# Down weights in whole 4 MB blocks, gate-up columns dealt to two column groups by eights

## The reference

```python
gu = jnp.dot(xb, w_gate_up[e]) + b_gate_up[e]          # 1024 -> 2048
glu = jnp.minimum(gu[:, ::2], SWIGLU_LIMIT)
lin = jnp.clip(gu[:, 1::2], -SWIGLU_LIMIT, SWIGLU_LIMIT)
act = glu * jax.nn.sigmoid(SWIGLU_ALPHA * glu) * (lin + 1.0)
y = jnp.dot(act, w_down[e]) + b_down[e]                 # 1024 -> 1024
```

## Time and profile before

| | |
|---|---|
| median of 3 runs | 1206.76 us (1205.69 to 1207.62) |
| the profiled execution | 1207.06 us, span 1205.3 us |
| mean granted clock of TensorE | 0.992 |
| TensorE busy / weight loads | 1148.6 us (95%) / 536.2 us |
| VectorE, ScalarE, GpSimd busy | 410.7, 208.5, 19.7 us |
| moved | 470.55 MB, mean 390 GB/s |
| chain that ended last | TensorE 68%, DMA 26%, VectorE 2% |

### The profile page before, as it was taken

One profiled execution on the slowest core, in us unless ns is written; L12 is line 12 of the kernel. 1 busy time (PEld: TensorE's weight loads), 2 busy tenths in 40 slices (PEclk: granted clock), 3 DMA queues, 4 the chain that ended last, 5 costly groups with the idle time before them and its releaser, 6 DMA issues.

```text
span 1205.3 us, 14952 instructions
## 1 busy us (share of the span) xinstructions
PE 1148.6 (95%) x6027; PEld 536.2 (44%) x6027; DVE 410.7 (34%) x798; ACT 208.5 (17%) x333; POOL 19.7 (2%) x40
## 2 busy tenths in 40 slices
PE   6999999999999999998989899999999999999997
PEld 4787889985333333332323233333333333333332
DVE  3547755673222232322222222222322323132222
ACT  3346644342010110101010101010101101010001
POOL 1000110000000000000000000000000000000000
PEclk9999999999999999999999999999999999999999
DMA  9997565699999999999999999999999999999994
GB/s 335 390 370 284 208 210 188 245 374 368 397 429 435 433 428 426 435 433 430 425 435 433 430 425 435 425 427 428 430 430 434 433 427 428 434 433 427 425 427 205
DMA packets 52546, 470.55 MB, mean 390 GB/s; under 512 B 4399, under 2 KB 9980, under 8 KB 31526
## 3 DMA queue, kind: packets, MB, share of 16 engines
q1 hardware_dynamic: 50308, 467.99, 93.5%
q10 hardware_dynamic: 2210, 2.16, 0.6%
HBM read 469.08 MB, written 1.06 MB: 390 GB/s over the span
## 4 chain that ended last, share of the span: by engine, by line
PE 68%; DMA 26%; DVE 2%; ACT 1%; issue 1%; SPq 1%; DVEq 0%; POOLq 0%; POOL 0%; ACTq 0%
PE ps L1059 22%; PE ps L828 15%; PE ps L1097 15%; DMA expert<-in_w_down 15%; DMA expert<-in_w_gate_up 11%; PE ps L1033 4%; PE ps L1004 2%; PE ps L772 2%; PE ps L703 1%; PE ps L985 1%; PE ps L1084 1%; ACT r_work L1299 1%; DMA ada_first<-in_w_ada 1%; DVE r_v L1740 1%; DVE r_v L1737 0%
## 5 line engine op out<-in xcount | busy, mean ns | idle before, releaser
L1059 PE MATMUL ps<-expert,r_work 128*64 128x512 f32 x2048 | 451.4, 595 | 7.4 <-DMA expert<-in_w_gate_up 6.6
L1059 PEld LDWEIGHTS ps<-expert,r_work 128*64 128x64 f32 x2048 | 147.1, 137 | 294.5 <-issue 281.4
L1097 PE MATMUL ps<-expert,r_work 128*64 128x512 f32 x1024 | 231.7, 603 | 23.4 <-DMA expert<-in_w_down 15.2
L1731 DVE TENSOR_SCALAR r_v<-ps 128x512 f32<-128x512 f32 x32 | 22.1, 692 | 366.4 <-PE ps L1059 366.4
L1097 PEld LDWEIGHTS ps<-expert,r_work 128*64 128x64 f32 x1024 | 72.7, 138 | 160.4 <-issue 135.8
L1295 ACT ACTIVATE r_v<-r_v 128x512 f32<-128x512 f32 x32 | 20.2, 630 | 706.5 <-DVE r_v L1731 706.5
L1408 DVE TENSOR_TENSOR w_lo<-stage,w_hi 128x2048 fp32r<-128x2048 f32 x36 | 82.8, 2306 | 55.3 <-ACT w_hi L1155 55.3
L1751 DVE TENSOR_TENSOR r_work<-ps,r_gb 64x512 f32<-64x512 f32 x64 | 44.1, 689 | 167.0 <-PE ps L1097 166.5
L828 PE MATMUL ps<-x_hi,w_hi 128*128 128x256 f32 x304 | 87.6, 288 | 0.0
L828 PE MATMUL ps<-x_lo,w_hi 128*128 128x256 f32 x304 | 86.0, 283 | 0.0
L828 PE MATMUL ps<-x_hi,w_lo 128*128 128x256 f32 x304 | 85.9, 283 | 0.0
(11 more groups left out here) (222 smaller groups left out, 866.5 us busy)
## 6 DMA issues: line engine op xcount, KB each, us to landing
expert<-in_w_gate_up SPq DMA_DIRECT2D x44, 4096.0 KB
expert<-in_w_down SPq DMA_DIRECT2D x64, 2048.0 KB, 18.4
expert<-in_w_gate_up SPq DMA_DIRECT2D x40, 2048.0 KB, 29.2
stage<-in_w_in SPq DMA_DIRECT2D x24, 1024.0 KB, 5.6
stage<-in_w_ada SPq DMA_DIRECT2D x16, 1024.0 KB, 7.1
ada_first<-in_w_ada SPq DMA_DIRECT2D x16, 256.0 KB, 6.4
ada_first<-in_w_ada SPq DMA_DIRECT2D x8, 512.0 KB, 11.9
stage<-in_w_o_attn SPq DMA_DIRECT2D x4, 1024.0 KB, 7.7
```

Source lines behind the costliest of these rows:

```text
L1059: mm = pe.matmul(ps[CAP * g:CAP * g + CAP, j, :], xg[:, 2 * (k % 4) + k // 4, :], buf[:, col:col + 512], start=False, stop=(k == KD - 1))
L1097: mm = pe.matmul(ps[CAP * half:CAP * half + CAP, 3, :], aT[:, ch, CAP * g:CAP * g + CAP], expert[n][:, col:col + 512], start=(q == 0), sto ...
```

## The change

The down weights of an expert are read with 32 KB runs in each partition: partition p now holds rows 8p to 8p + 7 of `w_down`, the first four in slot 4 and the last four in slot 5. In rounds 2 to 15 and 20 to 27 this is one load of 4 MB (`down_of_next`), issued when the whole down product of the round is done (`down_used` at 2i + 2); in the others two loads of 2 MB with runs of 16 KB stay, at their old moments. Both halves share one semaphore, and TensorE waits once, for all of the expert's down weights, before the first half of the product; the last expert alone keeps one semaphore for each half. In this row order group g must hold the features 8n + 4g + c, so the gate-up columns go to the groups by eights: the moving operand of a product is 64 runs of 8 neighbouring columns, 16 apart. The bias is loaded in the same order, which turns its runs of 512 columns into runs of 8. `rest_of_next` loses a branch that was never taken.

```diff
--- before.py
+++ after.py
@@ -142,6 +142,11 @@
 def dap(ap, offset, dims):
 
     return bass.AP(tensor=ap.tensor, offset=ap.offset + offset, ap=dims)
+
+
+def by_eights(ap, g):
+
+    return ap.rearrange("p (n g q) -> p g n q", g=2, q=8)[:, g]
 
 
 def backward(ap, blocks):
@@ -323,7 +328,8 @@
         first_landed = [sem(f"first{n}_landed") for n in range(KD)]
         stage_landed = [sem(f"stage{n}_landed") for n in range(WIDE)]
         block_landed = [sem(f"block{n}_landed") for n in range((NSLOT + TWICE) // 2)]
-        down_landed = [sem(f"down{n}_landed") for n in range(NSLOT - TWICE)]
+        down_landed = sem("down_landed")
+        last_down = [sem(f"last_down{n}_landed") for n in range(NSLOT - TWICE)]
         last_landed = [sem(f"last{n}_landed") for n in range(2 * TWICE)]
 
         ada_used, up_used, down_used = sem("ada_used"), sem("up_used"), sem("down_used")
@@ -385,9 +391,12 @@
             elif j % 2 == 0:
                 eng.wait_ge(block_landed[slot(j, parity) // 2], 32 * m + 32)
 
-        def wait_down(eng, j, i):
-
-            eng.wait_ge(down_landed[j - TWICE], 16 * i + 16)
+        def wait_down(eng, g, i, last):
+
+            if last:
+                eng.wait_ge(last_down[g], 16)
+            elif g == 0:
+                eng.wait_ge(down_landed, 32 * i + 32)
 
         def front_chunk(n):
 
@@ -445,7 +454,7 @@
 
                 n = slot(j, parity)
                 if j >= TWICE:
-                    landed = down_landed[j - TWICE]
+                    landed = last_down[j - TWICE] if last else down_landed
                 elif last:
                     landed = last_landed[TWICE * parity + j]
                 else:
@@ -454,8 +463,7 @@
                     d = 4 * P * (j // 2)
                     src = w_gate_up[0, e, d:d + 4 * P, :].rearrange("(p h k) n -> p h (k n)", h=2, k=2)[:, j % 2, :]
                 else:
-                    d = (j - UP_SLOTS) * 4 * P
-                    src = w_down[0, e, d:d + 4 * P, :].rearrange("(p k) n -> p (k n)", k=4)
+                    src = w_down[0, e].rearrange("(p g k) n -> p g (k n)", g=2, k=4)[:, j - UP_SLOTS, :]
                 sp.dma_start(expert[n][:, :], src).then_inc(landed, 16)
 
             def load_block(b, e, parity):
@@ -562,14 +570,17 @@
             final = sp.value_load(last_pair[0:1, 0:1], min_val=E // 2 - 1, max_val=ROUNDS * E // 2 - 1)
             ahead_of_final = sp.value_load(last_pair[0:1, 1:2], min_val=E // 2 - 2, max_val=ROUNDS * E // 2 - 2)
 
-            def rest_of_next(i, parity):
+            def rest_of_next(i, parity, last=False):
 
                 for j in range(TWICE, NSLOT):
-                    if j < UP_SLOTS:
-                        sp.wait_ge(up_used, UP_SLOTS * i + (j + 1))
-                    else:
-                        sp.wait_ge(down_used, 2 * i + (j - UP_SLOTS + 1))
-                    load_slot(j, (i + 1) % E, 1 - parity)
+                    sp.wait_ge(down_used, 2 * i + (j - UP_SLOTS + 1))
+                    load_slot(j, (i + 1) % E, 1 - parity, last)
+
+            def down_of_next(i):
+
+                sp.wait_ge(down_used, 2 * i + 2)
+                sp.dma_start(blocks[UP_SLOTS // 2][:, :],
+                             w_down[0, (i + 1) % E].rearrange("(p k) n -> p (k n)", k=8)).then_inc(down_landed, 32)
 
             def first_of_second(i, parity, last=False):
 
@@ -596,7 +607,7 @@
             with sp.Fori(1, CATCH_UP) as m:
                 for p in range(2):
                     blocks_of_second(2 * m + p, p)
-                    rest_of_next(2 * m + p, p)
+                    down_of_next(2 * m + p)
 
             for n in range(TWICE):
                 i, ahead = 2 * CATCH_UP + n, TWICE - n
@@ -606,12 +617,12 @@
 
             with sp.Fori(CATCH_UP + TWICE // 2, ahead_of_final) as m:
                 for p in range(2):
-                    rest_of_next(2 * m + p, p)
+                    down_of_next(2 * m + p)
                     blocks_of_second(2 * m + p, p)
             for p in range(2):
                 rest_of_next(2 * ahead_of_final + p, p)
                 first_of_second(2 * ahead_of_final + p, p, True)
-            rest_of_next(2 * final, 0)
+            rest_of_next(2 * final, 0, True)
             for n in range(2 * T):
                 t, cols = n // 2, slice(512 * (n % 2), 512 * (n % 2) + 512)
                 sp.wait_ge(y_out, n + 1)
@@ -1055,9 +1066,9 @@
                         buf = expert[slot(k // 2, p)]
                         for j in range(2):
                             for g in range(2):
-                                col = 2048 * (k % 2) + 1024 * g + 512 * j
+                                col = 2048 * (k % 2) + 1024 * j
                                 mm = pe.matmul(ps[CAP * g:CAP * g + CAP, j, :], xg[:, 2 * (k % 4) + k // 4, :],
-                                               buf[:, col:col + 512], start=False, stop=(k == KD - 1))
+                                               by_eights(buf[:, col:col + 1024], g), start=False, stop=(k == KD - 1))
                         if k % 2 == 1:
                             mm.then_inc(up_used, 1)
                     if p == 0:
@@ -1091,7 +1102,7 @@
                         g, ch = q // 4, q % 4
                         n = UP_SLOTS + g
                         if ch == 0:
-                            wait_down(pe, n, i)
+                            wait_down(pe, g, i, last and p == 1)
                         for half in range(2):
                             col = 1024 * ch + 512 * half
                             mm = pe.matmul(ps[CAP * half:CAP * half + CAP, 3, :], aT[:, ch, CAP * g:CAP * g + CAP],
@@ -1247,8 +1258,9 @@
 
                     act.wait_ge(ada_used, 3 * KD)
                     for r in range(4):
-                        act.dma_start(bgu[32 * r:32 * r + 32, :],
-                                      b_gate_up[0, :, 512 * r:512 * r + 512]).then_inc(late_landed, 16)
+                        act.dma_start(bgu[32 * r:32 * r + 32, :].rearrange("p (n q) -> p n q", q=8),
+                                      by_eights(b_gate_up[0, :, 1024 * (r % 2):1024 * (r % 2) + 1024], r // 2)
+                                      ).then_inc(late_landed, 16)
                     act.wait_ge(zeroed, 2)
                     act.dma_start(y2[0:E, :], b_down[0]).then_inc(late_landed, 16)
                 if p in (WO0, WO1) and n == LAST_CHUNK[p]:
```

## The result

The kernel with the change takes 1220.72 us (median of 4 runs, 1219.14 to 1223.01); the kernel before took 1207.19 us beside it (4 runs, 1205.69 to 1209.65). The ratio is 1.0112, 95% interval 1.0098 to 1.0125: 13.5 us slower, where +4.8 was forecast. The profiled execution took 1223.01 us with a span of 1221.2 us and a mean granted clock of 0.984 (0.992 before); it is 2.3 us above its median, so its rows show somewhat more than the median loses. Ratios are of runs made beside each other and need not be the quotient of the two medians to the last digit.

What follows compares the result with a forecast made beforehand. The weight stream was taken to bound the kernel while its queue never empties. An empty queue of 6.8 us less 2.0 from the rate gave +4.8 on 1206.76, 1211.6, given as 1211.5 us; range 1208.5 to 1217.

Steps and rivals of the forecast that it cites:

- What bounds the kernel, the rate: Expert stage: the weight stream decides while its queue never empties; 22 whole down blocks save 0.09 us each, 2.0 us.
- rival 5: Weight stream: each DMA's 2.8 us latency outside its transfer is paid in series; 22 fewer save 62 us, 1150; 1%.
- the 44 us: Weight stream: saving from 22 fewer DMAs if the skill page's some 2 us fixed cost each were paid in series.
- The wait and the issue at round 20: Waiting for both halves and issuing down only at T(20) leave the DMA queue empty 5.1 us, before any clock fall.
- the 0.4 us to spare: Round 2: the down block can start at 376.4, the queue lasts to 376.8 us; no cost taken, up to 1 us.
- The clock in round 17: TensorE's clock falls after a wait of about 3.6 us; T(17) and T(20) 1.7 us later, queue empty 6.8 us.
- rival 1: Round 20: the queue runs dry but the clock holds in round 17; +3.1 us, 1209.9; 27%.
- The columns: Gate-up products: reading columns in runs of eight with gaps costs nothing; upper bound 1.1 us a round.
- rival 3: Gate-up columns cost time each round: 1.1 us gives +7.3 more, 1219 (9%); half-speed reads about +410 us (1%).
- The bias: Front: four bias loads of 2048 short runs land in 34 us, inside 45 us of cover, issues stay 0.44 us; zero cost.
- Rival 4: Bias scatters into 8192 small packets, holding up the front by ACT's queue or the weights behind; +5 to +50 us; 3%.

Runs made afterwards that it cites:

- the spread bias: The changed kernel with its four bias loads issued at four chunks of the front (20 to 23) instead of all at chunk 20: 1212.81 us, ratio 1.0053.

## Why the prediction was wrong, point by point

- **What bounds the kernel, the rate:** right. A block takes 9.71 us and two pieces 9.80; the 22 blocks gave 1.9 us, not 2.0. Fixed costs in series (rival 5) are out: they would have given 62 us. The section of the page "DMA: Bandwidth & Descriptors" of the Trainium skill that the prediction cites fits its 2 us to DMAs issued by GpSimd, and these are issued by SP; the 44 us were therefore not what that section says of this kernel.
- **The wait and the issue at round 20:** right in place, mechanism and nearly in size. T(20) - T(17) is 83.3 us as said; the spell is 7.0 to 7.6 us for 6.8; the wait alone costs 5.3 us (3.7 expected by the same steps), the issue alone 2.8 (2.1). TensorE waited 2.4 us in round 17, where 3.6 was reckoned; T(17) came out 0.8 us later than forecast all the same (815.88 - 9.0 against 806.1). What was missed are the small gaps at round 2, where the 0.4 us to spare did not hold, and at round 19, which the prediction did not look at: 0.9 us together. Without the bias the change is at 1212.3 us (up to 7.4 us above the kernel before by the interval), the forecast was 1211.5.
- **The clock in round 17:** fell in the profile after, as the step had it, and did not in that of the spread bias; there the spell was 5.3 us instead of 7.0. Those 1.7 us are the step's own figure, so rival 1 and the forecast are two outcomes of the same kernel. Which one comes seems to hang on the rounds before. Rounds 15 and 17 of the kernel after, then of the one with the spread bias:

```profile
748.59 8.78 PE L1108 MATMUL ps<-expert,r_work 128*64 128x512 f32 x32 [3.47 <-DMA expert<-in_w_down]
...
738.62 9.52 PE L1108 MATMUL ps<-expert,r_work 128*64 128x512 f32 x32 [3.47 <-DMA expert<-in_w_down]
...
797.15 7.09 PE L1108 MATMUL ps<-expert,r_work 128*64 128x512 f32 x32 [1.74 <-DMA expert<-in_w_down]
```

  The fall cost round 15 0.7 us more in the second (9.52 against 8.78), so round 17 waited 1.74 us for its weights and not 2.44; there the clock held. In all the profiled kernels in which both halves are waited for in round 17 it fell there after 2.4 to 3.7 us of waiting (four) and held after 1.4 to 1.8 (three). The length of the wait does not settle it alone: in the kernel before waits of 2.0 to 2.1 us were followed by a fall in round 15 and by none in rounds 9, 11 and 13. It may be why the runs of these kernels spread over 5 to 6 us; only one execution of each was profiled.
- **The columns:** zero, as taken (rival 3 is out by the run of its own).
- **The bias:** this is the step that failed: "The four issues of 0.44 us stay: 32 and 1024 runs took the same." They became 10.4 us. The prediction asked when the data would land and who wants them (VectorE at 235.4, 45 us of cover), and costed that correctly at nothing; it did not ask what else stands in ScalarE's program behind the issues. That is the copy at L1191: it was due 3.3 us after the first issue (191.05 in the kernel before), and TensorE stood still 4 us after that. The row that it rested on, one issue of 1024 runs, could not show it: alone, an issue of 2048 is as cheap. Only in a row are they held, and the change had four in a row. The trace of the kernel before has such a case, on SP, at the line of the front's weight loads:

```profile
L531 SPq DMA_DIRECT2D stage<-in_w_ada x16: 327/340/3277, 30.0 to 157.2; - x16
```

  Most of these issues take 0.34 us; two, at 30 and 34 us, in a row in which each issue begins within 0.1 us of the last one's end, take 3.3 us. Rival 4 named the right place ("by ACT's queue") and its lower end, +5 us, was near, but got 3%; with a bound from the landing row (7.9 us for 1024 runs, four such in a row with the issuer held) it would have had a range of up to some 30 us (an estimate) and a larger chance. The sum was therefore some 8 to 9 us short: 4.8 + 8.8 = 13.6, against 13.5 measured. That these agree to 0.1 us is luck: the 8.8 has an interval of 5.8 to 10.4, and in the traces the bias is 7.7 us and the rest 6.6.

## What to carry to other kernels

A DMA with many short runs is paid by the engine that issues it and by everything behind it in that engine's program, not only by who waits for the data: look at what the issuer does next, and who needs that. Such loads can be issued one at a time, some microseconds apart; here that gave back 8 us (1220.72 to 1212.81) and cost nothing measurable. An engine with nothing due may do as well; that was not tried. And before two loads are made one in a stream that is the bound, follow the queue to the place where it is shortest: 22 blocks won 2 us, and one empty spell lost 7.

## What the runs showed of the hardware

- On ScalarE's queue an issue of 2048 runs of 32 bytes takes 0.32 to 0.35 us when the issue before it lies 6 us or more back, and 1.4 to 4.7 us right behind others; the small load after one of them took 3.16 us instead of 0.43.
- 8192 packets of 32 bytes, spread over 20 us, did not slow the 1 MB weight loads beside them measurably: 1212.81 us with them and 1212.29 without.
- TensorE, idle for 5.4 us in the front, went on at 1.2 GHz for some 5 us: of the 9.0 us by which T(0) is late, 1.3 were there before, 5.4 are the idle time and 2.5 the clock's (3.33 x 0.5 + 5 x 0.17, from the two stretches at 200 to 210 us), 9.2 in all.
- A moving operand read in runs of eight floats with gaps of eight is as fast as a contiguous one (593 and 595 ns; ratio 0.9997, 0.9987 to 1.0007).
